# Expert weights of an encoder layer: gate-up rows read in runs of 16 KB, slot groups of 32 in four column tiles

## What is computed

```python
gg, uu = jnp.split(xblk @ w_gu[e], 2, axis=-1)
return (jax.nn.silu(gg) * uu) @ w_dn[e]
```

## Time and profile before

| | us |
|---|---|
| median of three runs | 1088.45 |
| profiled execution | 1087.13 |
| its span, first to last instruction | 1085.3 |
| TensorE matmul busy | 1021.7 (94%) |
| ScalarE busy | 226.6 (21%) |
| VectorE busy | 208.4 (19%) |
| moved by DMA | 282.90 MB in 96353 packets |

### The profile page before, as it was taken

How to read it: one execution, slowest core, us unless ns; L and a number is a source line. 1 busy time by engine, 2 the same in 40 slices (tenths; PEclk the granted TensorE clock), 3 DMA queues, 4 the chain that set the end, 5 groups by cost and what they waited for, 6 DMA issues and landing times.

```text
span 1085.3 us, 11197 instructions
## 1 busy us (share of the span) xinstructions
PE 1021.7 (94%) x4596; PEld 631.3 (58%) x4596; DVE 208.4 (19%) x541; ACT 226.6 (21%) x399; POOL 19.1 (2%) x27
## 2 busy tenths in 40 slices
PE   5999999999999999999998999999999989888986
PEld 4888867878888888887486333333333333322332
DVE  1334102644031211012015311111110011100111
ACT  2421147641020000012112311111111111111112
POOL 1000000002000000100000000000000000000000
PEclk9999999999999999999998999999999999999999
DMA  9344432424444395444334399999999999999994
GB/s 320 116 148 150 153 132 101 155 78 156 155 180 149 121 378 219 155 155 155 114 119 175 132 395 409 409 409 410 410 409 410 410 409 410 410 410 409 409 410 174
DMA packets 96353, 282.90 MB, mean 261 GB/s; under 512 B 6273, under 2 KB 9025, under 8 KB 96321
## 3 DMA queue, kind: packets, MB, share of 16 engines
q1 hardware_dynamic: 89312, 279.03, 66.8%
q10 hardware_dynamic: 7008, 3.40, 1.2%
HBM read 281.37 MB, written 1.05 MB: 260 GB/s over the span
## 4 chain that ended last, share of the span: by engine, by line
PE 67%; SPq 27%; DMA 3%; issue 1%; DVE 1%; ACT 1%; DVEq 0%
PE bank L1172 41%; SPq L339 26%; PE bank L1456 7%; PE bank L1184 5%; PE bank L1477 4%; DMA blk<-in_w_gate_up_dram 2%; PE bank L1443 2%; PE bank L1432 1%; PE bank L1356 1%; PE bank L1376 1%; DMA prow<-in_norm_ffn_dram 1%; PE bank L1279 0%; PE bank L1425 0%; PE bank L1288 0%; SPq L345 0%
## 5 line engine op out<-in xcount | busy, mean ns | idle before, releaser
L1172 PE MATMUL bank<-blk,ring 128*128 128x256 f32 x2048 | 448.9, 381 | 3.3 <-DVE blk L911 1.5
L1172 PEld LDWEIGHTS bank<-blk,ring 128*128 128x128 f32 x2048 | 389.5, 191 | 59.8 <-issue 3.0
L1456 PE MATMUL bank<-ring,blk 128*64 128x512 f32 x768 | 175.1, 597 | 13.3 <-DMA ring<-in_w_gate_up_dram 11.7
L1456 PEld LDWEIGHTS bank<-ring,blk 128*64 128x64 f32 x768 | 56.7, 137 | 112.7 <-issue 98.1
L1477 PE MATMUL bank<-ring,cbm 128*64 128x512 f32 x384 | 87.7, 597 | 13.3 <-ACT cbm L674 13.3
L1110 DVE TENSOR_TENSOR cbm<-cbm,bank 128x256 f32<-128x256 f32 x32 | 13.5, 421 | 393.3 <-ACT cbm L671 393.3
L1443 PE MATMUL bank<-dec,blk 64*128 64x512 f32 x264 | 65.6, 615 | 0.7 <-ACT dec L677 0.7
L1477 PEld LDWEIGHTS bank<-ring,cbm 128*64 128x64 f32 x384 | 30.3, 137 | 55.2 <-issue 55.2
L671 ACT ACTIVATE cbm<-bank 128x256 f32<-128x256 f32 x32 | 12.3, 383 | 218.0 <-PE bank L1456 218.0
L1184 PE MATMUL bank<-ring,blk 128*128 128x512 f32 x128 | 55.8, 592 | 0.0
L527 ACT ACTIVATE blk<-bank 128x512 f32<-128x512 f32 x28 | 16.7, 597 | 169.1 <-PE bank L1172 169.0
(11 more groups left out here) (278 smaller groups left out, 607.1 us busy)
## 6 DMA issues: line engine op xcount, KB each, us to landing
ring<-in_w_gate_up_dram SPq DMA_DIRECT2D x48, 2048.0 KB, 23.5
ring<-in_w_down_dram SPq DMA_DIRECT2D x24, 2048.0 KB, 23.5
ring<-in_w_in_dram SPq DMA_DIRECT2D x20, 2048.0 KB, 8.0
params<-in_w_gate_up_dram SPq DMA_DIRECT2D x8, 2048.0 KB, 24.1
blk<-in_w_gate_up_dram SPq DMA_DIRECT2D x8, 2048.0 KB, 24.0
ring<-in_w_kv_dram SPq DMA_DIRECT2D x4, 2048.0 KB, 7.9
blk<-in_w_down_dram SPq DMA_DIRECT2D x4, 2048.0 KB, 24.0
params<-in_w_down_dram SPq DMA_DIRECT2D x4, 2048.0 KB, 24.1
```

The costliest lines, as they stand in the source:

```text
L1172: last = mm(ps[:, f * T:(f + 1) * T], w[:, k, c:c + P], src[:, k, :], start=k == 0, stop=k == KD - 1)
L1456: last = mm(gu_bank(p)[c * WIN:(c + 1) * WIN, :], xe[:, xin, 4 * j + k, :], w[:, k, :, c * SEG:(c + 1) * SEG], start=4 * j + k == 0, stop= ...
```

## The change

The gate-up weight is read with "(p k) n": partition p gets the rows 8p to 8p + 7, a half takes four neighbouring ones, so that a run is 16 KB, and runs lie 32 KB apart. The down weight is read as before. The features are laid on the partitions in the same way: the gather takes every eighth column of h3N for unit k, and the norm's weight comes in that order by a small load of its own (gffp, 12 loads become 13 in the list that ScalarE issues).

WIN is 32. Four column tiles of 32 take the place of two of 64: tile c takes 128 gate and 128 up columns, 256 moving columns instead of 512. The down projection has four tiles of 256 output columns, the scatter four tiles of 32 rows. There is one transpose of the hidden values instead of two. The banks x3 hold 256 output columns of both token tiles, where they held 512 of one. Square and norm at the end go over [2 x 1024] in one step each. The overflow plan counts further windows per expert with another formula (15 x 32 elements in its widest steps instead of 7 x 96).

```diff
-    WIN = 64
+    WIN = 32
+    NQ = P // WIN
...
+        gffp = sb("gffp", [P, KD])[:, :]
...
-        SEG = DE // 2
+        SEG = DE // NQ
+        COLS = D // NQ
...
-        hmT = cflat[:, 4 * SEG:6 * SEG].rearrange("p (b j c) -> p b j c", b=2, c=P)
-        yS = decflat[:, D:D + 512]
+        hmT = cflat[:, 4 * SEG:4 * SEG + 2 * P].rearrange("p (b c) -> p b c", b=2)
+        yS = decflat[:, D:D + COLS]
...
-        psum = [ctx.enter_context(nc.psum_tensor(f"bank{i}", [P, 512], F32)) for i in range(NB)]
+        banks = ctx.enter_context(nc.psum_tensor("bank", [P, NB, 512], F32))
+        psum = [banks[:, i, :] for i in range(NB)]
...
+        x3 = banks[:, 4:8, :].rearrange("p q (t n) -> p t q n", t=NT)
...
+                 (gffp, norm_ffn[0].rearrange("(p k) -> p k", k=KD))]
...
-                    src = w_gate_up[0, bass.ds(e, 1)].rearrange("a (k p) n -> p (a k) n", p=P)[:, 4 * j:4 * j + 4, :]
+                    src = w_gate_up[0, bass.ds(e, 1)].rearrange("a (p k) n -> p (a k) n", p=P)[:, 4 * j:4 * j + 4, :]
...
-                a.activation(slotsT[:, k, 0:SLOTS], ps[:, :], ACT.Copy, scale=col("gffn", k)).then_inc(read["ga"], 1)
+                a.activation(slotsT[:, k, 0:SLOTS], ps[:, :], ACT.Copy, scale=gffp[:, k:k + 1]).then_inc(read["ga"], 1)
...
-                a.copy(yS, down_bank[:, :]).then_inc(sem["yS_ready"], 1)
+                a.copy(yS, down_bank[:, 0:COLS]).then_inc(sem["yS_ready"], 1)
...
-            for i in range(2 * NT):
-                t, h = i // 2, i % 2
-                act.wait_ge(sem["x3_done"], i + 1)
-                last = a.activation(junk3[:, t, h * 512:(h + 1) * 512], x3_bank[i][:, :], ACT.Square,
-                                    accum_out=sq3[:, i:i + 1])
...
+            act.wait_ge(sem["x3_done"], NQ)
+            for t in range(NT):
+                last = a.activation(junk3[:, t, :].rearrange("p (q n) -> p q n", q=NQ), x3[:, t], ACT.Square,
+                                    accum_out=sq3[:, t:t + 1])
+            last.then_inc(sem["x3sq_ready"], 1)
+            act.wait_ge(sem["x3sq_ready"], 1)
+            a.activation(stat[:, 24:24 + NT], sq3[:, 0:NT], ACT.Sqrt, bias=epsc[:], scale=1.0 / D
+                         ).then_inc(sem["x3_rms"], 1)
...
-            big = ovf[0:1, 8 * NCAND:(8 + NOV) * NCAND].rearrange("p (o c) -> p o c", c=NCAND)
-            link(v.tensor_tensor(big, each(6), place, ALU.is_equal))
...
+            link(v.reduce_sum(more, ovm, AX.X))
+            v.tensor_tensor_scan(upto, ones[0:1, 0:NE], more, 0.0, ALU.mult, ALU.add)
...
+            link(v.tensor_tensor(ovf, every(upto),
+                                 iota_f[0:1, 0:NOV].rearrange("p (o e) -> p o e", e=1).to_broadcast([1, NOV, NE]),
+                                 ALU.is_le))
...
-                slots = iota_f[:, bass.ds(start, WIN)].rearrange("p (d w) -> p d w", d=1).to_broadcast([P, 2, WIN])
+                slots = iota_f[:, bass.ds(start, WIN)].rearrange("p (d w) -> p d w", d=1).to_broadcast([P, NQ, WIN])
...
+            dve.wait_ge(sem["x3_rms"], 1)
+            link(v.reciprocal(stat[:, 26:26 + NT], stat[:, 24:24 + NT]))
             for t in range(NT):
...
-                    v.scalar_tensor_tensor(out=outN[:, t, c], in0=x3_bank[2 * t + h][:, :], scalar=stat[:, 26 + t:27 + t],
-                                           in1=gfin[:, c], op0=ALU.mult, op1=ALU.mult).then_inc(sem["o_final"], 1)
+                    v.scalar_tensor_tensor(out=outN[:, t, c].rearrange("p (q n) -> p q n", q=NQ // 2),
+                                           in0=x3[:, t, h * NQ // 2:(h + 1) * NQ // 2], scalar=stat[:, 26 + t:27 + t],
...
-                mm(x3_bank[i][:, :], ident[:], x2N[:, t, h * 512:(h + 1) * 512], start=True, stop=False)
+            for q in range(NQ):
+                mm(x3_bank[q][:, :], ident[:], x2N[:, :, q * COLS:(q + 1) * COLS], start=True, stop=False)
...
-                    last = mm(ps[:, :], h3N[:, t, k * P:(k + 1) * P], sel[:, t, :], start=t == 0, stop=t == NT - 1)
+                    last = mm(ps[:, :], h3N[:, t, :].rearrange("p (f k) -> p k f", k=KD)[:, k, :], sel[:, t, :],
+                              start=t == 0, stop=t == NT - 1)
...
-                    for h in range(2):
-                        mm(x3_bank[2 * t + h][:, :], scat[h * WIN:(h + 1) * WIN, p, t * P:(t + 1) * P],
-                           yS[h * WIN:(h + 1) * WIN, :], start=False, stop=False)
+                    for q in range(NQ):
+                        mm(x3_bank[q][:, t * COLS:(t + 1) * COLS], scat[q * WIN:(q + 1) * WIN, p, t * P:(t + 1) * P],
+                           yS[q * WIN:(q + 1) * WIN, :], start=False, stop=False)
...
-                    w = slot(slots[j]).rearrange("p (k g n) -> p k g n", k=4, g=2)
+                    w = slot(slots[j]).rearrange("p (k g c m) -> p k g c m", k=4, g=2, c=NQ)
                     for k in range(4):
-                        for c in range(2):
-                            last = mm(gu_bank(p)[c * WIN:(c + 1) * WIN, :], xe[:, xin, 4 * j + k, :],
-                                      w[:, k, :, c * SEG:(c + 1) * SEG], start=4 * j + k == 0, stop=4 * j + k == KD - 1)
+                        for c in range(NQ):
+                            last = mm(gu_bank(p)[c * WIN:(c + 1) * WIN, 0:2 * SEG], xe[:, xin, 4 * j + k, :],
+                                      w[:, k, :, c, :], start=4 * j + k == 0, stop=4 * j + k == KD - 1)
...
-                for j in range(SEG // P):
-                    last = tp(turn_bank[:, j * P:(j + 1) * P], hm[:, p, j * P:(j + 1) * P], ident[:])
-                last.then_inc(sem["turn_done"], 1)
+                tp(turn_bank[:, 0:P], hm[:, p, :], ident[:]).then_inc(sem["turn_done"], 1)
...
-                    for h in range(2):
-                        last = mm(down_bank[h * WIN:(h + 1) * WIN, :], hmT[:, p, j, c * WIN:(c + 1) * WIN],
-                                  w[:, k, h * 512:(h + 1) * 512], start=k == 0, stop=k == NF - 1)
+                    for q in range(NQ):
+                        last = mm(down_bank[q * WIN:(q + 1) * WIN, 0:COLS], hmT[:, p, k * WIN:(k + 1) * WIN],
+                                  w[:, k, q * COLS:(q + 1) * COLS], start=k == 0, stop=k == NF - 1)
```

More of the change, by code:

```diff
@@ L1059, in _, with row @@
             link(v.memset(starts_i[0:1, NE:NE + 1], 0))
-            def ov(i, n=1):
-                return ovf[0:1, i * NCAND:(i + n) * NCAND]
+            def row(i, n):
+                return ovs[:, 32 * i:32 * i + n]
             st1, cnt1 = rv("st")[0:1, :], rv("cnt")[0:1, :]
[L1065 to L1068, removed]
-                last = v.tensor_copy(ov(3)[:, c], iota_f[0:1, 0:NE])
@@ L1070, in _ @@
-            link(last)
-            link(v.memset(ov(5), 1.0))
-            link(v.tensor_tensor_scan(ov(4), ov(5), ov(0), 0.0, ALU.mult, ALU.add))
-            link(v.tensor_tensor(ov(6), ov(4), ov(0), ALU.mult))
-            big = ovf[0:1, 8 * NCAND:(8 + NOV) * NCAND].rearrange("p (o c) -> p o c", c=NCAND)
-            big2 = ovf2.rearrange("p (o c) -> p o c", c=NCAND)
-            def each(i):
-                return ov(i).rearrange("p (o c) -> p o c", o=1).to_broadcast([1, NOV, NCAND])
-            place = iota_f[0:1, 1:NOV + 1].rearrange("p (o c) -> p o c", c=1).to_broadcast([1, NOV, NCAND])
@@ L1081, in _ @@
-            link(v.tensor_tensor(big, each(6), place, ALU.is_equal))
-            link(v.tensor_tensor(big2, big, each(3), ALU.mult))
-            link(v.reduce_sum(ov(7)[:, 1:NOV + 1], big2, AX.X))
-            link(v.tensor_tensor(big2, big, each(1), ALU.mult))
-            link(v.reduce_sum(ov(7)[:, NOV + 1:2 * NOV + 1], big2, AX.X))
-            link(v.tensor_copy(ov(7)[:, 0:1], ov(4)[:, NCAND - 1:NCAND]))
-            v.tensor_copy(ov_i[0:1, 0:2 * NOV + 1], ov(7)[:, 0:2 * NOV + 1]).then_inc(sem["ov_ready"], 1)
+            more, upto, rest, who, at, step_ = (row(0, NE), row(1, NE), row(2, NE), row(3, NOV), row(4, NOV), row(5, NOV))
@@ new lines, in _ @@
+            link(v.tensor_scalar(row(6, NMORE), iota_f[0:1, 1:NMORE + 1], float(WIN), None, ALU.mult))
+            link(v.tensor_tensor(ovm, cnt1.rearrange("p (e j) -> p e j", j=1).to_broadcast([1, NE, NMORE]),
+                                 row(6, NMORE).rearrange("p (e j) -> p e j", e=1).to_broadcast([1, NE, NMORE]),
+                                 ALU.is_gt))
+            link(v.reduce_sum(more, ovm, AX.X))
+            v.tensor_tensor_scan(upto, ones[0:1, 0:NE], more, 0.0, ALU.mult, ALU.add)
@@ new lines, in _, with every @@
+            link(v.scalar_tensor_tensor(out=rest, in0=more, scalar=-float(WIN), in1=cnt1, op0=ALU.mult, op1=ALU.add))
+            def every(ap):
+                return ap.rearrange("p (o e) -> p o e", o=1).to_broadcast([1, NOV, NE])
+            link(v.tensor_tensor(ovf, every(upto),
+                                 iota_f[0:1, 0:NOV].rearrange("p (o e) -> p o e", e=1).to_broadcast([1, NOV, NE]),
+                                 ALU.is_le))
+            v.reduce_sum(who, ovf, AX.X)
```

(14 more changed lines are left out.)

38 lines of the change are left out of this document (14 added, 24 removed).

## The result

The changed kernel takes 1073.39 us in the median of four runs (1072.6 to 1078.35), beside 1087.91 for the kernel before in runs of the same chip: a ratio of 0.9877, with a 95% interval of 0.9844 to 0.991. The profiled execution took 1073.69 us, its span is 1071.8 us, 13.5 less than the 1085.3 of before.

A forecast was written before the change was run, and what follows sets the result against it. It took the expert stage to be bound by DMA weight loads at a plateau of 409 to 410 GB/s. Terms 12.8 + 1.2 + 1.0 + 2.3 = 17.3 us off the 1088.45 median gave 1071, range 1064 to 1085.

The forecast's parts named there:

- Runs of 16 KB: Expert stage, 58 gate-up parts on the DMA path: 16 KB packets cut a part from 5.12 to 4.90 us, 12.8 us less.
- The start: Before the first refill: a quicker first half frees the weight slot sooner and the first token copy halves, 1.2 us less.
- The bubbles: From 620 to 640 us the DMA queue runs at 389 GB/s; quicker matmuls free slots sooner, 1.0 us less.
- The tail: From the last weight landing to the span's end: quicker down projection, copy and scatter, slightly slower norm, 2.3 us less.
- Costed at nothing: VectorE's overflow plan, ScalarE's new small load, the gather's strided weight tile and overflow windows: no time added.
- 1054 as a sign: End of the expert stage's DMA queue: the last weight part was to land near 1054 us.
- TensorE waits for DMA, also at 1.2 GHz: Expert stage: an expert takes TensorE about 10.5 us, near 14 at the lower clock, still hidden under 14.9 for its parts.
- The gather's strided load: Gather's weight tile with a stride of 8 elements: load 190 to 380 ns, sum unchanged; bound 10 us more.
- rival 1: Main DMA queue: packets don't get longer or the plateau is one of bytes; only 4.5 us gained, 1084; chance 0.22.
- issue-bound records: TensorE's matmul records limited to 0.116 us each, so halves gain nothing: 13.9 us gained, 1074.6; chance 0.08.
- long packets that run worse than their length: Gate-up DMA: 16 KB packets take 0.69 us, a part 5.52, so slower, 1107; chance 0.07.
- tiles that don't overlap: TensorE's four column tiles run one after another: a half 6.9 us, some 375 us slower; chance 0.02.

## Why the prediction was right, point by point

It said 1071 with a range of 1064 to 1085; measured were 1073.39. In the spans it forecast 17.3 us and 13.5 came: 0.7 less of the runs, 4.35 lost to a term that it doesn't have, and 1.3 more in the tail. That the time fell so near is in part luck, since the last two are errors that partly offset each other. By its steps, in the profiled executions:

- **Runs of 16 KB**, 12.8 us: right. 421 GB/s over 88 parts give 12.1, and 8 KB runs and long down runs fell on the same line (418 for 418, 427 for 428). The run with this half alone has the whole gain of the change, a ratio of 0.9877 for 0.9877. The page of the Trainium skill on the ports' ceiling (DMA: Bandwidth & Descriptors, "Where 436 GB/s comes from") was borne out so far: 427 GB/s, as a mean over 300 us, stayed under its 435.
- **The start**, 1.2 us: measured 1.2, by luck, as two errors offset. A record took 0.060 us and not 0.08, so the half was 1.93 for 2.6; the stages ahead ran 0.5 us longer (first expert at 610.36 for 609.83).
- **The bubbles**, 1.0 us: right, 424 GB/s in place of 389.
- **The tail**, 2.3 us: measured 3.6. The down projection took 1.98 for 2.6, the four closing matmuls 0.39 us in place of the 1.03 of before, and from the first square to the last product it was 5.46 us for 5.75; the scatter came as forecast (1.39 to the closing matmuls for 1.4). The record's pace was mis-sized, 0.08 for 0.060, near the lower bound of full overlap (0.053).
- **"Costed at nothing"** is the step that failed. It names VectorE's plan, ScalarE's load and the gather, but not the code of TensorE itself, whose loop grew from 120 to 230 records an expert. So the long body was put at nothing without a reason, and it cost 4.35 us by the sum above, about 5 like for like: 35 packets for 4. It is why the last part landed at 1059.3 where the prediction had named 1054 as a sign.
- **"TensorE waits for DMA, also at 1.2 GHz"**: right. The clock is at 0.82 in the mean from 740 to 1030, halves of up to 3.64 us, after waits of 2 to 3 us for the weights and stops of 5 for issue, stand beside such of 1.93, and the plateau is 421 GB/s for the 422 of the runs alone at full clock.
- **The gather's strided load**: it went from 190 to 313 ns and the gather stayed at 13.9 us, under its matmuls' 0.43 us. The Trainium skill's rule of the 16-byte line (SBUF — State Buffer, "Door 1: The DMA port swizzle") has its penalty here, and more plainly in the moving operand, where the stride of 16 bytes costs a factor of two. The load that the rule gave in the prediction, 380 ns, is above the 313 measured.
- **The rivals**: the packets got longer and the plateau rose with them, so rival 1 is out; so are issue-bound records (0.060 us each), long packets that run worse than their length (a gate-up part would have taken 5.52 us, and it took (438.4 - 30 x 5.12) / 58 = 4.91), and tiles that don't overlap.

## What to carry to other kernels

Where a stage is bound by DMA at a flat plateau, take the time of a packet apart into a fixed part and one per byte from two sizes that the trace has under a full queue; here the gain of longer runs followed from it to about a microsecond. Faster matmuls in such a stage bring only the start, the bubbles and the tail. And count the instructions of a loop body before unrolling or splitting them: code that is fetched again in each pass goes over the same DMA engines as the weights, and the transfer is complete when the slowest of them is. The mean of the plateau shows the smaller part of that; look at the last microseconds of the queue.

## What the runs showed of the hardware

- Four column tiles of 128 x 32 with 256 moving columns overlap nearly fully: 32 records in 1.93 us where a quarter of their time alone would be 1.74 (from 0.43 us for 512 columns), 0.060 us each, beside 0.228 for two tiles with 512.
- A loop body of TensorE of 960 records is fetched once (4 packets of 16 KB, 64 KB, for four passes), one of 460 too (2 packets for sixteen passes). Bodies of 1840 (eight experts in four tiles) and of 1920 (sixteen in two) are fetched again in each pass: 34 or 35 packets in four passes and 18 in two, 136 to 144 KB a pass. Where between 64 and 136 KB it turns, no run shows.
- A fetched packet in a full queue put the last landing off by 0.13 to 0.18 us.
- In the long body TensorE also stands still for issue, 15.4 us ahead of the gate-up records (three stops of about 5 us, which end at 703.8, 824.1 and 946.2; by the spacing, one to each new pass); with DMA as the bound this cost nothing that could be seen.
- A moving operand in float32 with a stride of four elements takes twice the time (7.33 for 3.65 us, 3.83 for 1.93); a weight load with a stride of eight elements 313 for 190 ns.
- With packets of 16 KB the queue takes more parts ahead: the last down part took 35 us from issue to landing, 29 with 8 KB and 24 with 4 KB, at a higher rate. A longer landing here is depth, not slowness.
